# Hybrid decoder trunk on one core: expert weights loaded in another order, first weights loaded by columns, first attention head loaded one stage earlier

## What is computed

```python
    def expert_block(args):
        xb, e = args
        return (jax.nn.silu(xb @ w1[e]) * (xb @ w3[e])) @ w2[e]

    ybuf = lax.map(expert_block, (buf.reshape(n_blocks, MOE_BLOCK, D), blk_e)).reshape(P, D)
```

## Time and profile before

| | us |
|---|---|
| median of three runs | 3083.65 (3083.41 to 3084.98) |
| profiled execution, its own time | 3087.63 |
| its span in the trace | 3086.0 |
| project_qkv, from its first transfer issue | 3.35 to 348 |
| gate stage | 349 to 601 |
| attention | 601 to 1121 and its tail |
| run_experts | 2026 to 2990 |
| PE busy over the span | 2699.6 (87%) |
| mean granted TensorE clock | 0.935 of full |

### The profile page before, as it was taken

How to read it: one execution, slowest core, us unless ns; L and a number is a source line. 1 busy time by engine, 2 the same in 40 slices (tenths; PEclk the granted TensorE clock), 3 DMA queues, 4 the chain that set the end, 5 groups by cost and what they waited for, 6 DMA issues and landing times. The chain is left out here.

```text
span 3086.0 us, 47061 instructions
## 1 busy us (share of the span) xinstructions
PE 2699.6 (87%) x14218; PEld 2246.1 (73%) x14219; DVE 1541.6 (50%) x1973; ACT 1330.9 (43%) x2388; POOL 531.9 (17%) x621
## 2 busy tenths in 40 slices
PE   6999599699999979978899999379988999999960
PEld 4888488589999867767688888357766788878750
DVE  3222255377777762221333333456777755565537
ACT  3222233188888861101322222035666644554522
POOL 1000011266666640000000000000000000000013
PEclk9999799899999989989999999669989999999985
DMA  5444411233222222241212221057888766676739
GB/s 178 149 148 148 157 48 61 70 72 72 51 48 51 48 82 92 102 184 62 91 69 80 77 82 62 34 205 271 315 330 319 293 228 238 242 257 218 267 149 366
DMA packets 215357, 463.99 MB, mean 150 GB/s; under 512 B 38656, under 2 KB 71936, under 8 KB 213248
## 3 DMA queue, kind: packets, MB, share of 16 engines
q1 hardware_dynamic: 192544, 380.34, 36.1%
q0 software_dynamic: 15984, 58.20, 5.1%
q10 hardware_dynamic: 6768, 24.64, 2.0%
HBM read 363.50 MB, written 99.61 MB: 150 GB/s over the span
## 5 line engine op out<-in xcount | busy, mean ns | idle before, releaser
L717 POOL TENSOR_TENSOR stick_weight<-stick_weight,stick_left 128x512 f32<-128x512 f32 (+3 forms) x320 | 330.6, 1043 | 187.1 <-DVE stick_left L842 184.8
L1877 DVE TENSOR_TENSOR moe_w_lo<-moe_w_lo_raw,moe_w_hi (+1 forms) x256 | 302.3, 1221 | 109.1 <-ACT moe_w_hi L1822 95.0
L1822 ACT CAST moe_w_hi<-moe_w_lo_raw (+1 forms) x256 | 261.3, 1050 | 126.3 <-DMA moe_w_lo_raw<-in_w 98.8
L842 DVE TENSOR_TENSOR_SCAN stick_left<-stick_z_ps,stick_left,stick_any_row 128x512 f32<-128x512 f32 x192 | 246.0, 1281 | 76.7 <-ACT stick_z_ps L808 75.7
L787 PE MATMUL stick_o_ps<-stick_v,stick_weight_t 128*128 (+1 forms) x2176 | 280.0, 268 | 3.9 <-ACT mix_yb L820 3.3
L787 PEld LDWEIGHTS stick_o_ps<-stick_v,stick_weight_t 128*128 128x128 f32 x2176 | 268.0, 192 | 8.7 <-ACT mix_yb L820 4.2
L806 ACT ACTIVATE stick_weight<-stick_z_ps 128x512 f32<-128x512 f32 (+3 forms) x320 | 173.1, 541 | 78.6 <-PE stick_z_ps L770 41.7
L58 PE MATMUL moe_g_ps<-moe_w_hi,moe_x_hi 128*128 x376 | 162.4, 432 | 32.6 <-DVE moe_w_lo L1877 20.3
L778 PE MATMUL stick_t_ps<-all_ident,stick_weight 128*128 128x128 f32 x1088 | 171.9, 273 | 0.6 <-POOL stick_weight L717 0.6
L58 PE MATMUL qkv_z_ps<-qkv_w_hi,qkv_h_hi 128*128 128x512 f32 x384 | 156.7, 408 | 18.0 <-DVE qkv_h_lo L238 18.0
L808 ACT ACTIVATE stick_z_ps<-stick_z_ps 128x512 f32<-128x512 f32 (+3 forms) x320 | 165.7, 518 | 10.1
(11 more groups left out here) (282 smaller groups left out, 6060.9 us busy)
## 6 DMA issues: line engine op xcount, KB each, us to landing
moe_w_lo_raw<-in_w SPq DMA_DIRECT2D x512, 256.0 KB, 7.7
moe_w_lo_raw<-in_w SPq DMA_DIRECT2D x128, 512.0 KB, 6.8
y_scratch<-moe_y ACTq DMA_DIRECT2D x47, 512.0 KB, 7.4
y_scratch<-qkv_zeros POOLq DMA_DIRECT2D x31, 512.0 KB, 5.6
qkv_xs<-in_x SPq DMA_DIRECT2D x16, 512.0 KB, 5.2
qt_scratch<-qkv_q_t SPq DMA_DIRECT2D x16, 512.0 KB, 3.2
kt_scratch<-qkv_k_t SPq DMA_DIRECT2D x16, 512.0 KB, 3.5
gmlp_xs<-in_x SPq DMA_DIRECT2D x16, 512.0 KB, 3.4
```

Source lines behind the costliest of these rows:

```text
L717: nc.gpsimd.tensor_tensor(taken, taken, left[:, i % LEFTS, c * BANK + 1:c * BANK + keys + 1], ALU.mult).then_inc(weight_done, 1)
L842: nc.vector.tensor_tensor_scan(left[:, i % LEFTS, c * BANK:c * BANK + keys][:, ::-1], back, any_row[:, 0:keys], start, ALU.mult, ALU.bypas ...
L1822: nc.scalar.copy(w13_hi[:, w13_at(e, i)], w13_raw[:, w13_at(e, i)]).then_inc(w13_cut, 1)
L1877: nc.vector.tensor_tensor(w13_lo[:, w13_at(e, i)], w13_raw[:, w13_at(e, i)], as_f32(w13_hi[:, w13_at(e, i)]), ALU.subtract).then_inc(w13_r ...
```

## The change

Three parts.

1. **Start.** `set_constants` and its barrier are gone; POOL writes the constants at the head of its list in `project_qkv`, and PE waits for them. `w_in` is loaded as three column blocks (q, k, v) of eight 256 KB transfers each, straight into the place where the low part will stand (`two_views`), so SP waits for no buffer. ACT issues the load of the gains. ACT and DVE cut the q columns, then make h of tile 0, then cut the k and v columns. PE waits row by row for the cut in all three products of tile 0.
2. **First head.** The buffers of q, k and v are allocated before the gate stage (`StickLoads`), and SP issues the ten loads of head 0 in the gate stage, behind the loop and ahead of the last four stores.
3. **Experts.** SP's list: w13 of experts 0 and 1, w2 of 0; then w13 of 2, w2 of 1, w13 of 3, w2 of 2 and so on. w2 of expert e-1 now waits for the y products up to expert e-3.

```diff
         w_hi = s.sbuf("w_hi", [P, rows, cols], F32R)
-        w_lo = s.sbuf("w_lo", [P, rows, cols], F32R)
-        w_raw = s.sbuf("w_raw", [P, RAW, cols])
+        w_lo, w_raw = s.two_views("w_lo", [P, rows, cols])
...
-                sp.dma_start(gains[:], gain.partition_broadcast(P)).then_inc(gains_loaded, 16)
-
                 def load_x(t, slot):
                     sp.dma_start(xs[:, slot], x[bass.ds(t * P, P), :]).then_inc(x_loaded[slot], 16)
 
+                def load_w(c):
+                    for r in range(rows):
+                        sp.dma_start(w_raw[:, r, c * BANK:(c + 1) * BANK],
+                                     w_in[r * P:(r + 1) * P, first_col + c * BANK:first_col + (c + 1) * BANK]).then_inc(w_loaded[c][r], 16)
+
                 load_x(0, 0)
+                load_w(0)
                 load_x(1, 1)
-                for r in range(rows):
-                    if r >= RAW:
-                        sp.wait_ge(w_lo_done, r - RAW + 1)
-                    sp.dma_start(w_raw[:, r % RAW], w_in[r * P:(r + 1) * P, first_col:]).then_inc(w_loaded[r % RAW], 16)
+                load_w(1)
+                load_w(2)
...
+                nc.gpsimd.memset(ident[:], 0.0).then_inc(filled, 1)
+                nc.gpsimd.memset(half[:], -0.5).then_inc(filled, 1)
+                nc.gpsimd.memset(ident_bf[:], 0.0).then_inc(filled, 1)
+                nc.gpsimd.memset(above[:], 0.0).then_inc(filled, 1)
+                pool.wait_ge(filled, 4)
+                for tile, compare, fill in ((ident, ALU.not_equal, 1.0), (ident_bf, ALU.not_equal, 1.0), (above, ALU.is_gt, -1e30)):
+                    nc.gpsimd.affine_select(out=tile[:], in_=tile[:], compare_op=compare, fill=fill, base=0,
+                                            pattern=[[-1, P]], channel_multiplier=1).then_inc(masked, 1)
                 nc.gpsimd.memset(zeros[:], 0.0).then_inc(zeroed, 1)
...
+                def cut_w(c):
+                    for r in range(rows):
+                        act.wait_ge(w_loaded[c][r], 16)
+                        nc.scalar.copy(w_hi[:, r, c * BANK:(c + 1) * BANK], w_raw[:, r, c * BANK:(c + 1) * BANK]).then_inc(w_hi_done, 1)
+
+                act.dma_start(gains[:], gain.partition_broadcast(P)).then_inc(gains_loaded, 16)
                 square(0, 0)
-                for r in range(rows):
-                    act.wait_ge(w_loaded[r % RAW], 16 * (r // RAW + 1))
-                    nc.scalar.copy(w_hi[:, r], w_raw[:, r % RAW]).then_inc(w_hi_done, 1)
+                cut_w(0)
                 high_h(0, 0)
+                cut_w(1)
+                cut_w(2)
...
+                def cut_w(c):
+                    for r in range(rows):
+                        dve.wait_ge(w_hi_done, c * rows + r + 1)
+                        cut = slice(c * BANK, (c + 1) * BANK)
+                        nc.vector.tensor_tensor(w_lo[:, r, cut], w_raw[:, r, cut], as_f32(w_hi[:, r, cut]), ALU.subtract).then_inc(w_lo_done, 1)
+
                 norm(0, 0)
-                for r in range(rows):
-                    dve.wait_ge(w_hi_done, r + 1)
-                    nc.vector.tensor_tensor(w_lo[:, r], w_raw[:, r % RAW], as_f32(w_hi[:, r]), ALU.subtract).then_inc(w_lo_done, 1)
+                cut_w(0)
                 low_h(0, 0)
+                cut_w(1)
+                cut_w(2)
...
                     for r in range(rows):
                         if cutting:
-                            pe.wait_ge(w_lo_done, r + 1)
+                            pe.wait_ge(w_lo_done, chunk * rows + r + 1)
...
+                pe.wait_ge(masked, 3)
                 transpose_h(0, 0)
...
-                    product(slot, 1, zk_done)
+                    product(slot, 1, zk_done, cutting=first_tile)
...
-                    product(slot, 2, zv_done)
+                    product(slot, 2, zv_done, cutting=first_tile)
...
                 pair(0, True)
                 with sp.Fori(1, tiles // 2 - 1) as j:
                     pair(j, False)
+                first_head.load_q(sp, qt, 0, 0)
+                first_head.load_kv(sp, kt, v, 0)
+                for g in range(1, first_head.q_groups):
+                    first_head.load_q(sp, qt, 0, g)
                 for t in range(tiles - 4, tiles):
                     store(t, t % 2)
...
+class StickLoads:
+
+
+    def __init__(self, s, heads, head_dim, tokens):
+        self.head_dim, self.tokens, self.tiles, self.q_groups = head_dim, tokens, tokens // P, tokens // BANK
+        self.q_sb = s.sbuf("q", [P, tokens], F32R)
+        self.k_hi = s.sbuf("k_hi", [P, 2 * tokens], F32R)
+        self.k_lo = s.sbuf("k_lo", [P, 2 * tokens], F32R)
+        self.v_sb = s.sbuf("v", [P, 2 * self.tiles * head_dim])
+        self.kv_loaded = s.sem("kv_loaded")
+        self.q_loaded = [s.sem(f"q_loaded{g}") for g in range(self.q_groups)]
+
+    def load_kv(self, sp, kt, v, h):
+        d, tiles = self.head_dim, self.tiles
+        for to, part in ((self.k_hi, 0), (self.k_lo, d)):
+            for side in range(2):
+                sp.dma_start(as_f32(to[side * d:(side + 1) * d, bass.ds((h % 2) * self.tokens, self.tokens)]),
+                             kt[bass.ds(h, 1), part:part + d, :].rearrange("o p t -> (o p) t")).then_inc(self.kv_loaded, 16)
+        sp.dma_start(self.v_sb[:, bass.ds((h % 2) * tiles * d, tiles * d)].rearrange("p (n d) -> p n d", n=tiles),
+                     v.rearrange("(n p) c -> p n c", p=P)[:, :, bass.ds(h * d, d)]).then_inc(self.kv_loaded, 16)
+
+    def load_q(self, sp, qt, h, g):
+        cut = slice(g * BANK, (g + 1) * BANK)
+        sp.dma_start(as_f32(self.q_sb[:, cut]), qt[bass.ds(h, 1), :, cut].rearrange("o p t -> (o p) t")).then_inc(self.q_loaded[g], 16)
...
-                load_q(0, 0)
-                load_kv(0)
-                for g in range(1, tiles // per):
-                    load_q(0, g)
                 def load_next(h, first):
                     if not first:
                         sp.wait_ge(av_done, h * n_units)
                     sp.wait_ge(kv_loaded, 80 * (h + 1))
-                    load_kv(h + 1)
+                    loads.load_kv(sp, kt, v, h + 1)
                     for g in range(tiles // per):
                         sp.wait_ge(z_done, h * n_units + group_end[g])
-                        load_q(h + 1, g)
+                        loads.load_q(sp, qt, h + 1, g)
...
                 for i in range(rows):
                     load_w13(0, i)
-                for i in range(h_rows):
-                    load_w2(0, i)
                 for i in range(rows):
                     sp.wait_ge(w13_loaded[i], 32)
                     load_w13(1, i)
                 for i in range(h_rows):
-                    sp.wait_ge(w2_loaded[i], 16)
-                    load_w2(1, i)
-                with sp.Fori(2, experts) as e:
-                    blocks = blocks_before(e - 1)
-                    sp.wait_ge(up_done, blocks)
+                    load_w2(0, i)
+
+                def next_w13(e):
+                    sp.wait_ge(up_done, blocks_before(e - 1))
                     sp.sem_inc(w13_free, 1)
                     for i in range(rows):
                         sp.wait_ge(w13_loaded[i], 32 * e)
                         load_w13(e, i)
-                    sp.wait_ge(y_done, blocks)
-                    sp.sem_inc(w2_free, 1)
+
+                def next_w2(e, first):
+                    if not first:
+                        sp.wait_ge(y_done, blocks_before(e - 1))
+                        sp.sem_inc(w2_free, 1)
                     for i in range(h_rows):
                         sp.wait_ge(w2_loaded[i], 16 * e)
                         load_w2(e, i)
+
+                next_w13(2)
+                next_w2(1, True)
+                with sp.Fori(3, experts) as e:
+                    next_w13(e)
+                    next_w2(e - 1, False)
+                next_w2(experts - 1, False)
...
-                set_constants(nc, ident, half, ident_bf, above)
-                project_qkv(nc, x[0], norm_mix[0], w_in[0], ident[:], half, qt, kt, v, ybuf[experts * P:, :])
-                mix_chunks(nc, x[0], norm_mix[0], w_in[0], v_norm[0], w_spatial[0], b_spatial[0], out_norm_a[0], ident[:], half, ya)
+                project_qkv(nc, x[0], norm_mix[0], w_in[0], ident[:], half, ident_bf, above, qt, kt, v, ybuf[experts * P:, :])
+                first_head = StickLoads(m, heads, head_dim, tokens)
+                mix_chunks(nc, x[0], norm_mix[0], w_in[0], v_norm[0], w_spatial[0], b_spatial[0], out_norm_a[0], ident[:], half, ya,
+                           qt, kt, v, first_head)
                 yb = m.sbuf("yb", [P, tiles, half_width])
-                attend_stick(nc, qt, kt, v, ident[:], ident_bf[:], above[:], yb)
+                attend_stick(nc, qt, kt, v, first_head, ident[:], ident_bf[:], above[:], yb)
```

(14 more changed lines are left out.)

33 lines of the change are left out of this document (3 added, 30 removed).

## The result

The changed kernel takes **3001.27 us** (median of four runs, 2999.75 to 3002.47) where the kernel before, measured beside it, takes 3083.68: ratio 0.9732, 95% interval 0.9715 to 0.9749. It is 82.4 us faster; 99 were forecast.

A forecast was written before the change was run, and what follows sets the result against it. PE, busy 87% of the span, was taken as the bound, leaving only its idle stretches to win. Experts 78 + first head 12 + start 9 = 99 us, from 3083.65 to 2984.6 us; range 2972 to 3008.

The forecast's parts named there:

- the full range: Whole kernel: the range of 8 in 10 for its time, 2972 to 3008 us.
- rival 1: Experts' stage: transfers become the bound of one-block experts, 18.95 us against steps of 18.09; 2995 to 3008 us, chance 0.15.
- The nine long steps: Experts' stage: nine steps of 24.55 to 29.78 us against 18.09, w13 issued 10.2 us behind release; 80.6 us in all.
- What is late next?: Experts' stage: once long steps go, only transfers run late, w13's cut has 9 us slack; 78 us credited.
- Transfers: Experts' stage: one-block experts' transfers take 18.95 us against 18.09, falling 0.86 us behind per expert; 2.6 us charged.
- First head, 12 us: Start of attention: the load wait goes, POOL's fills become the wait; first scan 10.4 us earlier, 12 us credited.
- Start, 9 us: Start of first projection: second product begins at 29.9 in place of 40.36; 9 us credited, between 6 and 12.
- Rival 2: Experts' stage: queues average only 358 GB/s, an expert's transfers take 20.6 us; 3017 us, chance 0.03.
- Rival 3: Experts' stage: long steps stay, set by another wait of ACT or DVE; only 21 us won, 3063 us, chance 0.06.
- Rival 4: Experts' stage: w2, issued behind the next expert's w13, comes too late for PE's y product; 3260 us, chance 0.02.

The follow-up runs named there:

- the split wait: Changed kernel, PE waiting for rows 0 to 5 of the w13 cut before the g product, for rows 6 and 7 only before row 6: 2987.84 us.
- the split wait and the late w13: Changed kernel with PE's wait for the w13 cut split and the y wait put back ahead of w13: 2990.84 us.

## Why the prediction was right, and where it was not

The sign, the size of two terms out of three, and the cause of the long steps were right; the forecast of 2984.6 was 16.7 us too low. The time lies outside the 2973 to 2995 of "the forecast itself", which had a chance of 0.74, and inside the full range only because that reaches into the times of rival 1, whose cause did not act. That it lies inside is to that extent luck.

- **The nine long steps.** Right. The nine h waits are gone, in the changed kernel and with the experts' part alone. What was said to cost them was that "SP then still stood at the y wait of the set before"; the runs narrow it: not the wait but the w2 that it held, standing ahead of w13.
- **What is late next?** This is the step that failed. "All rows at 13.5, the last cut 2.3 us later, 15.8" against "PE wants them at 18.09 + 7 = 25", and so a slack of 9 us, takes DVE as free when w13 lands. Measured: the last cut ends 26.4 us behind the release, because DVE has the cut of w2 (4.63), six rows of w13 (6.90), the h product and the low half of x in front of the last two rows. All of these durations stood in the trace of before; they were not laid end to end. The cost is seven waits of 1.6 us, 13.1 us of the stage, and the split wait, which touches only that, gives 13.4 back.
- **Transfers.** That they "run behind by 0.86 us per expert" was right in kind and twice too big: 0.39 measured, since the queues moved 398 to 399 GB/s over 90 us where the 3 us window had shown 389. The 2.6 us charged for it are 0.7 in the kernel with the split wait (two steps of 18.39 and 18.53) and nothing in the changed kernel, whose steps of 19.03 us on average are longer than the 18.5 that the transfers need.
- **First head, 12 us.** The fifth sigmoid came 8.83 us behind the stage's first fill in place of 21.06, 12.2 us less; the stage is 11.5 us shorter. The scan stood where it was put: 7.43 us behind the first fill, 7.5 forecast.
- **Start, 9 us.** Second product at 29.5, forecast 29.9. The gate stage begins 9.5 us earlier, and the start alone gave 8.6.
- **Rival 1** gave the time (2995 to 3008) for another reason: the transfers bound nothing in the changed kernel. With the split wait and the late w13 they do, at 18.5 us a step. Rival 2 (358 GB/s) falls with the windows of 390 and 399. Rival 3 named "another wait of ACT or DVE" and was told off by ACT's row; DVE's row of before, where PE's wait at L58 was put down to `moe_w_lo`, was read as part of the same delay. It was a cause of its own, as the kernel before with the split wait shows. Rival 4: no wait of PE for w2 appears.
- The profiled execution of before stood 4.0 us above its median, and that was carried through the sum as if the difference were the same in both. By the spans the forecast of 99 was 11.5 too high, by the medians 16.6.

The Trainium skill, "DMA: Bandwidth & Descriptors", "Where 436 GB/s comes from", puts the bound of transfers between HBM and SBUF at about 358 GB/s; by that rule, as an estimate, an expert's 7.37 MB take 20.6 us. The windows disagree: 398 and 399 GB/s over 90 us with this one core at work. The Trainium skill, same page, "Measured", asks for transfers of 1 MiB and more to reach 75% of the peak. At the start transfers of 256 KB, with the 512 KB of x tile 1 among them, stood behind each other and moved 388 GB/s, more than the 341 that it gives for 1 MB (window of the changed kernel):

```profile
3.00:21.00 18.00, 7.22 (x20) 5.70 (x21) 12.79 (x22) 13.42 (x23) 0.92 (x2) 1.00 1.03 388
```

## What to carry to other kernels

Where a late transfer is taken away, write out the list of every engine that works on its data, from the last point at which that engine truly waits, and add the durations up to the product that needs them: the next bound is in that sum, and its terms are in the trace of before. A wait for a whole set, where the first rows would do, cost 1.6 to 3 us a time here as soon as the set was just in time; splitting it gained 13.4 us, and the reordering of ACT's list that was tried against it lost 6.8. Before you move an item to start another one sooner, look at which item that one truly follows.

## What the runs showed of the hardware

A somewhat longer wait of PE cost more than its length. In the changed kernel PE waits 1.6 us and the stretch is granted the full clock. With ACT's order changed it waits 2.12 to 2.18 us; three of the seven steps last 20.53 us and four about 22.05. The two windows are a step of either kind; the rows below are from the longer one's g product, those of line 58 alone, every third matmul.

```profile
2125.44:2145.96 20.52, 18.36 (x86) 14.77 (x84) 18.63 (x20) 15.92 (x20) 1.59 (x2) 1.00 1.04 399
2164.05:2186.14 22.09, 19.91 (x85) 15.94 (x84) 20.20 (x21) 15.94 (x20) 1.61 (x2) 0.92 1.03 399
```
```profile
2174.36 0.63 PE L58 MATMUL moe_g_ps<-moe_w_hi,moe_x_hi 128*128 x1
2175.64 0.63 PE L58 MATMUL moe_g_ps<-moe_w_hi,moe_x_hi 128*128 x1
...
2178.44 0.40 PE L58 MATMUL moe_g_ps<-moe_w_hi,moe_x_hi 128*128 x1
2179.14 0.40 PE L58 MATMUL moe_g_ps<-moe_w_hi,moe_x_hi 128*128 x1
```

Three matmuls take 1.28 us behind the wait, 0.70 later: the lower of the two levels, 1.2 GHz, and then 2.4 GHz. Between 2174 and 2180 the granted clock is 0.73. The drop adds 1.5 us to a wait of 2.2, but only in four cases of seven, and in none of the seven at 1.6 us. The length of the wait doesn't decide it: the one of 2.12 us is followed by a drop, one of the two of 2.18 is not. What decides stays open.
